# One block for the tail of the token mixing and the output projection

## The reference, cut to what matters

```python
o = head_layernorm(o_sum, lp['rwkv_ln_g'].reshape(H_A, HD_A))
bonus = jnp.sum(rh * kh * lp['rwkv_rk'], axis=-1, keepdims=True) * vh
out_a = (o + bonus).reshape(B, T, W_A) * g                        # RWKV heads: 256 channels
out_b = rmsnorm(o, lp['diff_subln_g'], eps=1e-5) * (1.0 - lam_init)  # attention: 512 channels
out_c = h_sum * jax.nn.gelu(gc, approximate=False)                # RG-LRU: 256 channels
y = jnp.concatenate([out_a, out_b, out_c], axis=-1) @ lp['w_out']
sh1, sc1, g1, sh2, sc2, g2 = jnp.split(jax.nn.silu(cond) @ w + b, 6, axis=-1)
x = x + g1 * y
h2 = rmsnorm(x, lp['norm2_g']) * (1.0 + sc2) + sh2
```

## Time and profile before

| what | us |
|---|---|
| three runs, median | 4262.58 |
| the profiled execution, its own time | 4262.3 |
| its span, first to last instruction | 4260.5 |
| first layer: end of the mixing's last DVE work to the last residual add of the projection | 632.5 to 736.8 |
| second layer: the same stretch | 2721.6 to 2825.8 |

### The profile page before, as it was taken

The page is one execution under the profiler, slowest core; times in us unless marked ns, Lnnn a source line. Parts: engine busy times, 40 slices in busy tenths (PEclk is TensorE's granted clock), DMA queues, the critical chain, the costliest instruction groups (busy, mean ns, idle before and its releaser), DMA issues. The chain is left out here.

```text
span 4260.5 us, 69584 instructions
## 1 busy us (share of the span) xinstructions
PE 3985.3 (94%) x25862; PEld 3144.3 (74%) x25862; DVE 3344.0 (78%) x6323; ACT 1531.9 (36%) x2428; POOL 1430.4 (34%) x1046
## 2 busy tenths in 40 slices
PE   7989988999998999999979899789999899999997
PEld 4976766655567888888879677585555688888885
DVE  2547754699998999999845666538999899999996
ACT  4425533311164333333353355331112633333333
POOL 0010000165414656666400000004644066566661
PEclk8988998999999999999989799799999999999998
DMA  6221003699999999999721300237999999999994
GB/s 248 70 92 47 2 9 116 213 380 328 357 293 365 408 394 398 403 407 403 294 90 55 128 2 2 91 114 283 356 341 321 298 400 403 397 404 407 403 405 167
DMA packets 412893, 1096.10 MB, mean 257 GB/s; under 512 B 38240, under 2 KB 183904, under 8 KB 405984
## 3 DMA queue, kind: packets, MB, share of 16 engines
q1 hardware_dynamic: 265184, 555.88, 36.3%
q0 software_dynamic: 147456, 536.94, 32.4%
HBM read 1013.25 MB, written 79.43 MB: 256 GB/s over the span
## 5 line engine op out<-in xcount | busy, mean ns | idle before, releaser
L1748 POOL DMA_INDIRECT ring<-peer_u_rows,rows x512 | 672.4, 1313 | 1822.0 <-DVEq L2102 1127.3
L1748 POOL DMA_INDIRECT ring<-peer_v,rows x512 | 733.3, 1432 | 431.7 <-DVE acc L2565 360.6
L1705 PE MATMUL ps<-h,u 128*128 128x384 f32 x2048 | 676.7, 487 | 2.5 <-PEq L1821 2.5
L2565 DVE SCALAR_TENSOR_TENSOR acc<-ring,act,acc 128x1024 f32<-128x1024 f32 x508 | 644.5, 1283 | 0.8
L1752 DVE SCALAR_TENSOR_TENSOR ring<-ring,acc 128x1024 f32<-128x1024 f32 x512 | 614.7, 1223 | 11.1 <-DMA ring<-peer_u_rows,rows 10.9
L205 PE MATMUL ps<-vhi,wlo 128*128 128x512 f32 x1536 | 602.2, 392 | 20.9 <-DVE wlo L2544 20.1
L206 PE MATMUL ps<-vlo,whi 128*128 128x512 f32 x1536 | 598.7, 390 | 0.0
L207 PE MATMUL ps<-vhi,whi 128*128 128x512 f32 x1536 | 598.6, 390 | 0.0
L1705 PEld LDWEIGHTS ps<-h,u 128*128 128x128 f32 x2048 | 382.5, 190 | 252.0 <-issue 2.9
L2530 DVE TENSOR_TENSOR vlo<-v,vhi 128x1024 fp32r<-128x1024 f32 x256 | 313.5, 1225 | 75.8 <-ACT vhi L2472 75.6
L205 PE MATMUL ps<-xhi,ulo 128*128 128x384 f32 x1024 | 344.9, 337 | 23.1 <-DVE xlo L2522 23.1
(11 more groups left out here) (359 smaller groups left out, 7184.0 us busy)
## 6 DMA issues: line engine op xcount, KB each, us to landing
u<-peer_u SPq DMA_DIRECT2D x256, 512.0 KB, 6.8
v<-peer_v SPq DMA_DIRECT2D x256, 512.0 KB, 6.5
gates<-stage SPq DMA_DIRECT2D x24, 2048.0 KB, 10.3
sel<-gates SPq DMA_DIRECT2D x64, 768.0 KB, 7.5
mod_ring<-mod_late SPq DMA_DIRECT2D x32, 1024.0 KB, 7.4
query_raw<-peer_wq SPq DMA_DIRECT2D x64, 512.0 KB, 4.5
hidden<-hh SPq DMA_DIRECT2D x128, 192.0 KB, 7.3
u<-hidden SPq DMA_DIRECT2D x128, 192.0 KB, 6.6
```

The costliest lines, as they stand in the source:

```text
L1705: mm = pe.matmul(self.g.ps[:, bank, 0:ND], self.u[:, slot, kc, :], self.x[:, kc, 0:ND], start=(kc == 0), stop=(kc == KC - 1))
L1748: return pool.indirect_dma_start(to, None, table, rows)
L2565: ve.scalar_tensor_tensor(acc, r, w, acc, ALU.mult, ALU.add).then_inc(used, 1)
```

## The change

mix_finish, gemm and split_programs go; one function, tail_stage, makes a single block of them. What it does:

- mix_stage no longer waits for its state stores; the new block's ACT waits for them, ahead of its third weight block, and SP at its end.
- The head sums alternate between the bank pairs 6-7 and 4-5. ACT takes the logarithms straight from PSUM (scale 1/64 and the epsilon as a bias from the new tile eps), so DVE's six copies (L1640) are gone. The function table natural_log_exp_and_others is loaded by hand at the start.
- The order of the chunks in the products becomes 6, 7 (recurrent unit), 2 to 5 (attention), 0, 1 (RWKV). Raw weights come through a ring of three, split weights through a ring of four, sums through three bank pairs. The first three columns go chunk by chunk: columns 0 and 1 take chunks 6 and 7 first, then column 2 takes them when its banks 4-5 are free of the bonus sums and its weights are split, then all three go on together.
- Late modulation piece i is multiplied after column 3 + i, and the turn of piece i - 1 follows it; its sums have one bank (6), its ring two halves, its buffers lie in free chunks of the tile proj. On SP's queue the loads stand in the order: weights 0 to 2, piece 0, weights 3 to 5, piece 1, weights 6 and 7, piece 2.
- The part of mod_shifts that the residual needs is made early, the rest after the seventh column's residual add.

```diff
@@ mix_stage
             for h in range(2):
                 rows = slice(h * HD, (h + 1) * HD)
                 sync.dma_start(d["new_rwkv"][l, h], sz[rows, :, :, h * HD:(h + 1) * HD]).then_inc(stored, 16)
-            sync.wait_ge(stored, 32)
...
+    return stored
@@ Modulation
     def sums(self, pe, i):
-        if i >= 2:
-            pe.wait_ge(self.row, i - 1)
+        ahead = len(set(self.banks[0:2]))
+        if i >= ahead:
+            pe.wait_ge(self.row, i + 1 - ahead)
@@ tail_stage
+TAIL_RING = 4
+TAIL_RAW = 3
+TAIL_SUMS = 3
+CHUNKS = [CA + CB, CA + CB + 1, *range(CA, CA + CB), *range(CA)]
...
         @block.sync
         def _(sync):
-            mod.load(sync, range(NLATE - MODS_FIRST))
+            def load(n):
+                if n >= R:
+                    sync.wait_ge(w_lo, n - R + 1)
+                sync.dma_start(raw[:, n % R, :, :], d["w_out"][l, n]).then_inc(w_in[n % R], 16)
+
+            for n in range(R):
+                load(n)
+            mod.load(sync, range(1))
+            for n in range(R, 2 * R):
+                load(n)
+            mod.load(sync, range(1, 2))
+            for n in range(2 * R, KC):
+                load(n)
+            mod.load(sync, range(2, mod.n))
+            sync.wait_ge(states_stored, 32)
...
             for c in range(CA):
-                sum_heads(MEANS + c, g.outT[:, c, :])
-            for c in range(CB + CA):
+                sum_heads(c, g.outT[:, c, :])
+            for c in range(CB):
                 pe.wait_ge(sq, c + 1)
-                sum_heads(SQUARES + c, s[:, c, :])
+                if c < CA:
+                    pe.wait_ge(centred, c + 1)
+                else:
+                    pe.wait_ge(logs, c + 1 - CA)
+                sum_heads(SQ + c, s[:, c, :])
+            for c in range(CA):
+                pe.wait_ge(rec_sq, c + 1)
+                pe.wait_ge(logs, CB - CA + c + 1)
+                sum_heads(REC + c, s[:, CB + c, :])
             for c in range(CA):
                 pe.wait_ge(bonus, c + 1)
+                pe.wait_ge(logs, CB + c + 1)
                 sum_heads(BONUS + c, bo[:, c, :])
-            for i in range(mod.n + 1):
-                mod.on_tensor(pe, i)
...
+            pe.wait_ge(w_lo, S - 1)
+            for p in range(CC):
+                pe.wait_ge(low, p + 1)
+                for n in range(S - 1):
+                    for h in range(2):
+                        chunk(n, h, CHUNKS[p])
+            pe.wait_ge(w_lo, S)
+            pe.wait_ge(bonus_tk, CA)
+            for p in range(CC):
+                for h in range(2):
+                    chunk(S - 1, h, CHUNKS[p])
+            for p in range(CC, KC):
+                pe.wait_ge(low, p + 1)
+                for n in range(S):
+                    for h in range(2):
+                        mm = chunk(n, h, CHUNKS[p])
+                    if p == KC - 1:
+                        mm.then_inc(ready, 1)
+            for n in range(S, KC):
+                pe.wait_ge(w_lo, n + 1)
+                pe.wait_ge(taken, n - S + 1)
+                for h in range(2):
+                    for kc in CHUNKS:
+                        mm = chunk(n, h, kc)
+                mm.then_inc(ready, 1)
+                if n - S <= mod.n:
+                    mod.on_tensor(pe, n - S)
...
+            nc.scalar.preload_act_table_set("natural_log_exp_and_others")
             for c in range(CB):
                 nc.scalar.activation(s[:, c, :], g.outT[:, CA + c, :], ACT.Square).then_inc(sq, 1)
...
+            for c in range(CA):
+                log(c)
+            for kc in CHUNKS[0:CC]:
+                out_high(kc)
+            for n in range(2):
+                w_high(n)
+            for c in range(CA, CB):
+                log(c)
+            for c in range(CA):
+                root(c)
+            for c in range(CB, CB + CA):
+                log(c)
+            for c in range(CB, CB + CA):
+                root(c)
+            for c in range(CA, CB):
+                root(c)
+            act.wait_ge(states_stored, 32)
+            w_high(2)
+            for c in range(CB):
+                act.wait_ge(scaled, c + 1)
+                out_high(CA + c)
+            for c in range(CA):
+                act.wait_ge(rec_done, c + 1)
+                out_high(c)
+            for n in range(S, 2 * S + 1):
+                w_high(n)
+            mod.on_scalar(act, 0)
+            w_high(KC - 1)
+            for i in range(1, mod.n + 1):
                 mod.on_scalar(act, i)
...
+            mod_shifts(g, Counter(ve, early), g.modL[:, 0:KC, :], 2 * KC, KC, None)
+            for p in range(CC):
+                out_low(p)
+            for n in range(2):
+                w_low(n)
+            for c in range(CA):
+                attention(c)
             for c in range(CA):
                 ve.wait_ge(sums, BONUS + c + 1)
-                ve.tensor_tensor(bo[:, c, :], flat(BONUS + c), g.proj[:, V0 + c, :], ALU.mult).then_inc(taken, 1)
+                ve.tensor_tensor(bo[:, c, :], flat(BONUS + c), g.proj[:, V0 + c, :], ALU.mult).then_inc(bonus_tk, 1)
...
+            w_low(2)
+            for c in range(CA):
+                out_low(CC + c)
...
+            w_low(S)
+            take = residual_take(g, 2)
+            for n in range(KC):
+                ve.wait_ge(ready, n + 1)
+                take(ve, n, g.ps[:, 2 * (n % S):2 * (n % S) + 2, 0:H2]).then_inc(taken, 1)
+                if n + W < KC:
+                    w_low(n + W)
+                if n == KC - 2:
+                    ve.wait_ge(mod.taken, mod.n)
+                    mod_shifts(g, Counter(ve, late), g.modL[:, KC:, :], 3 * KC, 3 * KC, (1, "n2", 4))
@@ build
-                    mix_stage(g, l, keep)
-                    mix_finish(g, l, keep)
-                with ExitStack() as s2:
-                    out2 = [g.sb(s2, f"out{x}", [P, KC, NT], F32R) for x in ("hi", "lo")]
-                    gemm(g, "wout", lambda oc: dram["w_out"][l, oc], KC, 4, 2, out2, residual_take(g, 2),
-                         lambda st: split_programs(g, "out", g.outT, *out2))
+                    states_stored = mix_stage(g, l, keep)
+                tail_stage(g, l, gt, states_stored)
```

More of the change, by code:

```diff
@@ L207, in split3 @@
     return pe.matmul(out, lhs[0], rhs[0], start=False, stop=stop)
[L210 to L262, removed]
-            def chunk(j, h, kc):
-                w = (hi[:, j % SR, kc, :], lo[:, j % SR, kc, :])
-                return split3(pe, g.ps[:, 2 * j + h, 0:H2], w, [x[:, kc, h * H2:(h + 1) * H2] for x in rhs],
-                              start=(kc == 0), stop=(kc == KC - 1))
-            def column(i, j):
-                pe.wait_ge(w_lo, i * R + (j + 1 + R))
-                pe.wait_ge(taken, i * R + (j + 1))
-                for h in range(2):
-                    for kc in range(KC):
-                        mm = chunk(j, h, kc)
-                mm.then_inc(ready, 1)
-            pe.wait_ge(w_lo, SR + R)
-            for kc in range(KC):
-                pe.wait_ge(before["chunk_low"], kc + 1)
-                for j in range(SR):
-                    for h in range(2):
-                        mm = chunk(j, h, kc)
-                    if kc == KC - 1:
-                        mm.then_inc(ready, 1)
-            for j in range(SR, R):
-                column(0, j)
-            with pe.Fori(0, n_out // R - 1) as i:
-                for j in range(R):
-                    column(i + 1, j)
-        @block.vector
-        def _(ve):
-            ve.sem_inc(taken, R)
-            def low(i, j):
-                i, j = i + j // R, j % R
-                ve.wait_ge(w_hi, i * R + (j + 1))
-                s = j % SR
-                ve.tensor_tensor(lo[:, s, :, :], raw[:, j, :, :], hi[:, s, :, :].bitcast(F32), ALU.subtract).then_inc(w_lo, 1)
-            def turn(i, last):
-                for j in range(R):
-                    ve.wait_ge(ready, i * R + (j + 1 + SR))
-                    take(ve, i * R + j, g.ps[:, 2 * j:2 * j + 2, 0:H2]).then_inc(taken, 1)
-                    if not (last and j + SR >= R):
-                        low(i, j + SR)
-            before["vector_first"](ve)
-            for j in range(SR):
-                low(0, j)
-            before["vector"](ve)
-            with ve.Fori(0, n_out // R - 1) as i:
-                turn(i, False)
-            turn(n_out // R - 1, True)
@@ L363, in turn @@
         for c in range(MP // P):
-            mm = pe.matmul(self.g.ps[:, 7, 2 * c:2 * c + 2], self.rows[:, i % 2, c * P:(c + 1) * P], self.g.groups[:, :],
+            mm = pe.matmul(self.g.ps[:, self.banks[2], 2 * c:2 * c + 2], self.rows[:, i % 2, c * P:(c + 1) * P], self.g.groups[:, :],
                            start=True, stop=True)
@@ L371, in take_row @@
             act.wait_ge(self.turned, i - 1)
-        self.g.nc.scalar.activation(self.rows[:, i % 2, :], self.g.ps[:, 5 + i % 2, :], ACT.Copy).then_inc(self.row, 1)
```

(1 more changed line is left out.)

139 lines of the change are left out of this document (82 added, 57 removed).

## The result

| what | before | after |
|---|---|---|
| median of the runs, us | 4263.49 (four runs, 4261.6 to 4265.92) | 4218.97 (four runs, 4215.29 to 4228.24) |
| the profiled execution, its own time | 4262.3 | 4222.62 |
| its span | 4260.5 | 4220.7 |
| tail, first layer: scan's end to last residual add | 104.3 | 92.05 |
| tail, second layer | 104.0 | 92.24 |

A forecast was written before the change was run, and what follows sets the result against it. The projection's 384 matmuls on PE were taken as the tail's floor, with gains ahead of them. Tail 10.8, store wait 1.5 and norm 1.3 make 13.6 us a layer, 27.2 in two: 4262.3 - 27.2 = 4235.1 us, range 4223 to 4251.

The forecast's parts named there:

- 4262.3 - 27.2: Whole kernel: the profiled execution's time less 13.6 us gained in each of two layers, giving 4235.1 us.
- the bounds of the unknown terms: Tail and norm: start 16.6 to 19.8, clock 0 to 5, norm 0 to 1.3; forecast said 4226 to 4249.
- clock holds: Rival, tail: PE keeps 2.4 GHz through both waits, 4.4 us more gained a layer, 4226; chance 0.14.
- Store wait: Scan's end to tail block: it ends when the second store is issued, not landed; gain 1.5 us a layer.
- First product: Tail's start: first projection product 18.0 us after the block's start, between 16.6 (clock kept) and 19.8 (clock lost).
- Products and modulation between columns: Projection: 384 matmuls 56.3 us, 0.4 lost at column 2, three modulation pieces and turns 8.6 us on the path.
- The new wait: Ahead of modulation piece 1: PE stands still 2.7 us for its row, behind ACT's copy of weight 6.
- The clock in it: PE's idle time ahead of modulation piece 1 may drop it to 1.2 GHz: 0 to 5 us, 3.0 taken.
- Norm: Next norm: the table load between logarithm and exponential goes, 0 to 1.3 us a layer, 1.3 taken.
- Tables not shared: Rival, tail and norm: loads return at each logarithm-exponential turn, 6.4 us less gained a layer, 4248; chance 0.10.
- Given back: Rival, tail: table and clock losses at once with slower landings leave 2 us gain a layer, 4258; chance 0.09.
- slower by half clock through the projection: Rival, projection: clock falls and stays, matmuls 0.267 not 0.147 us, 15 us a layer slower, 4293; chance 0.05.

The follow-up runs named there:

- e2: The kernel before plus only the new tile eps, filled once and unused: 4249.37 us, ratio 0.9968.
- e8: The changed kernel with the wait for the two state stores put back at the end of the recurrent scan's block: 4219.22 us, ratio 0.9910.
- e4: The changed kernel with weights 6 and 7 ahead of modulation piece 1 on SP's queue: 4204.76 us, ratio 0.9863.
- e6: The changed kernel without the by-hand load of the table of logarithms and exponentials: 4242.41 us, ratio 0.9944.
- e3: The changed kernel without the new tile, the epsilons kept in free columns of the tile tiny: 4238.15 us, ratio 0.9944.

## Why the prediction missed

**What failed is the sum's base.** "4262.3 - 27.2" takes every stage outside the tail and the norm as unchanged, because no line of them is in the diff. The diff's line for eps is in all of them. The row that would have carried a term is not among those I read: DMA share 1.00 in 809 us of experts and 1.03 in 116 us of gates, where any change of a transfer's rate is a change of the time. What the runs showed in its place: 12.6 us from the tile alone (e2), and in the traces 4.3 us a layer in the experts and 3.2 in the gates. The range was too narrow for it, although its upper end was generous: the bounds of the unknown terms add up to 4226 to 4245 (10.2 us above the forecast), not to 4249. Of the rivals none had this: the likely "clock holds" gave a time near the result, 4226, by another mechanism, which the traces do not show (in the first layer the clock fell in both waits: it stood at 0.50 from 643.9 to 645.9 and averaged 0.66 from 690 to 695).

**The steps of the tail**, in us, first layer (second behind it where it differs):

| step | forecast | measured |
|---|---|---|
| store wait and meeting | 1.5 gained | 1.3 (3.4 to 2.1) |
| first head sum to first product | 18.0 (16.6 to 19.8) | 17.7; 16.5 |
| columns 0 to 3, half of 56.3, with 0.4 lost | 28.6 | 28.8 |
| from there to the last add's end: half of 56.3, 8.6, 2.7, 3.0, 1.2 | 43.6 | 43.4; 44.9 |
| first head sum to last add's end | 90.2 | 90.0; 90.2 |
| norm | 1.3 gained | 1.0 (16.9 to 15.9, last add's end to the first chunk scaled) |

That the whole meets 90.2 in both layers is in part luck, since the errors of the two clock terms and of the new wait partly cancel.

*Store wait:* right at its joint; whether it reaches the end is open (e8).

*First product:* the walk of ACT's list is right, the price of the clock too high. The changed kernel's ACT between the logarithms and the roots has no load, where the earlier trace rows has one:

```profile
642.73 1.47 ACT L1580 ACTIVATE proj<-ps,eps 128x640 f32<-128x640 f32 x2
644.08 1.36 ACT L1584 ACTIVATE proj<-proj 128x640 f32<-128x640 f32 x2
...
648.35 2.61 ACT L1584 ACTIVATE proj<-proj 128x640 f32<-128x640 f32 x4
```

The wait for the third logarithm was 2.3, with 2.6 expected. In the second layer the clock held through it (0.87 over the stretch) and the first product came at 16.5, as the bound of 16.6 said. In the first it fell (0.77) and the product came at 17.7, where the bound for that case was 19.8; that the 18.0 between them is near 17.7 is luck.

*Products and modulation between columns:* right. Three bank pairs, a ring of four split weights and the late pieces cost what their matmuls cost. Residual adds that frame a column with a modulation piece and a turn (702.78 to 712.76) and a column with a turn only (712.76 to 720.76):

```profile
702.78 1.14 DVE L1695 SCALAR_TENSOR_TENSOR xT<-ps,modT,xT 128x320 f32<-128x320 f32 x3 [7.79 <-PE ps L207]
712.76 1.13 DVE L1695 SCALAR_TENSOR_TENSOR xT<-ps,modT,xT 128x320 f32<-128x320 f32 x3 [8.84 <-PE ps L207]
720.76 1.14 DVE L1695 SCALAR_TENSOR_TENSOR xT<-ps,modT,xT 128x320 f32<-128x320 f32 x3 [6.33 <-PE ps L207]
```

9.98 is 7.04 + 1.82 + 1.05 and 0.07 more; 8.00 is 7.04 + 1.05 within 0.1.

*The new wait:* right in place and cause, mis-sized: 3.5 for 2.7. Weight 6 was there 9.8 us after piece 1's first half was issued (679.65 to 689.45), where the sum had 5.0, 2.6 and 1.3, 8.9. The first half landed after 5.0 as reckoned; the second, issued 0.9 later, landed 3.6 behind it and not 2.6:

```profile
DMA to landing us min/median/max: 5.0/6.3/7.7
```

*The clock in it:* 1.7 in the first layer and 3.2 in the second, for 3.0; both are what e4 gave back beyond the 3.5. With the wait that is 5.2 and 6.7 for 5.7.

*Norm:* the load between logarithm and exponential is gone, as the earlier trace rows had it:

```profile
735.41 0.74 ACT L358 ACTIVATE sel<-sel 128x640 f32<-128x640 f32 x1 [7.17 <-DVE sel L381]
736.17 0.74 ACT L360 ACTIVATE sel<-sel 128x640 f32<-128x640 f32 x1
737.80 3.00 ACT L365 ACTIVATE h<-h,modT,gain 128x512 f32<-128x512 f32 x5 [0.89 <-DVE h L391]
```

Before, the first chunk was scaled at:

```profile
753.73 0.81 ACT L466 ACTIVATE h<-h,modT,gain 128x512 f32<-128x512 f32 x1 [0.89 <-DVE h L492]
```

The Trainium skill, "ScalarE: Activation LUTs", section "Table sets: the hidden batching unit", says that one set holds both functions; the changed kernel and e6 now show it. The further drain that its section "What ACT_TABLE_LOAD costs" counts is not seen: with its load the norm's exponential began 1.29 us after the load's start in e6 too, the norm of e6 is 1.3 us longer than the changed kernel's (17.2 to 15.9), and the change gave 1.0, not 2.7.

**The rivals.** Tables not shared: false for the change, true without its one line, and under-priced (8.6 and 8.4 a layer, not 6.4), since more time also went by at 1.2 GHz behind the first product. Given back, and slower by half clock through the projection: neither; columns 0 to 3 run at 1.00, and the one fall among the late columns of each layer costs 1.7 and 3.2; in the second layer the clock was back behind it (0.72 from 2755 to 2767, then 1.00 to the end). Without the tile the time fell where the forecast had it (e3, 4238.15), so what missed is outside the tail.

## What to carry to other kernels

A diff that allocates anything in an outer frame moves every tile allocated after it, and can change stages that it does not touch: before costing the stage that is edited, see where the tiles of the DMA-bound stages begin before and after, and give such a shift a term of its own. Test it by the tile alone, unused, in the old kernel; otherwise its gain is credited to the edit. And a load queued behind another load's ring wait inherits that wait: ask for the weights that the next operation needs ahead of those that must wait for a buffer.

## What the runs showed of the hardware that was not expected

- Where a tile begins on a partition changes the rate of its transfers: the 2 MB gate transfers took 8.2 to 8.5 us from multiples of 256 bytes and 10.3 to 10.6 from any other start that was tried (32, 64, 128 and 224 bytes beyond); in stages with the DMA engines full this was 0.3 to 0.5% of the kernel.
- A wait put back can cost less than its length by way of the clock: with the store wait (e8) the head sums began 1.3 us later in both layers, and the next 16 us ran at a mean of 0.90 of 2.4 GHz, where the changed kernel had 0.77 in one layer and 0.87 in the other. The first product came 0.5 us sooner after the scan's end in the first layer and 0.8 later in the second; at the end of the tails it was 0.4 sooner and 2.6 later, so no gain is shown.
